# Sums of squares in column halves on GpSimd, the middle statistic one weight unit later, and the last out-projection tile earlier in VectorE's order

## The reference

```
y = xf * lax.rsqrt(jnp.mean(xf * xf, axis=-1, keepdims=True) + RMS_EPS)
x = x + 0.5 * (jax.nn.silu(h @ w_gate) * (h @ w_up)) @ w_down      # h = y * g
```

## Time and profile before

| what | value |
|---|---|
| runs of the kernel | 1577.7, 1579.8, 1580.04 us; median 1579.8 |
| the profiled execution's own time | 1578.12 us |
| its span in the profile | 1576.3 us |
| granted clock, mean | 0.976 of full speed |
| TensorE busy | 1486.0 us (94%), 7230 matmuls |
| VectorE, ScalarE, GpSimd busy | 569.3, 508.9, 765.7 us |

### The profile page before, as it was taken

One profiled execution on the slowest core, in us unless ns is written; L12 is line 12 of the kernel. 1 busy time (PEld: TensorE's weight loads), 2 busy tenths in 40 slices (PEclk: granted clock), 3 DMA queues, 4 the chain that ended last, 5 costly groups with the idle time before them and its releaser, 6 DMA issues.

```text
span 1576.3 us, 20170 instructions
## 1 busy us (share of the span) xinstructions
PE 1486.0 (94%) x7230; PEld 1229.4 (78%) x7230; DVE 569.3 (36%) x794; ACT 508.9 (32%) x706; POOL 765.7 (49%) x1013
## 2 busy tenths in 40 slices
PE   5796999999999999999999999689999999999997
PEld 5674888888888788888888687578867888888887
DVE  6796342222002832222000746934544322221003
ACT  4425333333123333222212674022233332232112
POOL 0373465555555655554555636260045654555553
PEclk9898999999999999999999999879999999999999
DMA  8871234322232222322322222000022322223221
GB/s 316 320 267 41 94 133 147 106 93 94 95 105 80 94 95 91 106 93 93 104 96 94 71 76 72 14 1 1 1 67 81 134 85 101 94 92 106 94 80 54
DMA packets 44545, 156.90 MB, mean 100 GB/s; under 512 B 4944, under 2 KB 7376, under 8 KB 44240
## 3 DMA queue, kind: packets, MB, share of 16 engines
q1 hardware_dynamic: 44496, 156.22, 28.6%
HBM read 154.11 MB, written 2.10 MB: 99 GB/s over the span
## 4 chain that ended last, share of the span: by engine, by line
PE 78%; issue 9%; DVE 7%; POOL 4%; ACT 1%; DVEq 0%; POOLq 0%; ACTq 0%
PE ps L1562 23%; PE ps L1564 23%; PE ps L1563 23%; POOL w_lo L458 4%; DVE act_lo L1031 1%; DVE tri_p L1028 1%; DVE tri_x L1028 1%; PE ps L1922 1%; DVE xT L1031 1%; PE ps L1978 1%; DVE mid_sq L1031 0%; PE ps L1929 0%; PE ps L1935 0%; PE ps L1876 0%; PE ps L1982 0%
## 5 line engine op out<-in xcount | busy, mean ns | idle before, releaser
L458 POOL TENSOR_TENSOR w_lo<-raw,w_hi 128x256 fp32r<-128x256 f32 x932 | 698.2, 783 | 723.5 <-ACT w_hi L623 653.8
L1562 PE MATMUL ps<-act_hi,w_hi 128*128 128x512 f32 x1328 | 526.4, 396 | 15.9 <-DVE act_lo L1028 11.4
L1563 PE MATMUL ps<-act_lo,w_hi 128*128 128x512 f32 x1328 | 518.6, 391 | 0.0
L1564 PE MATMUL ps<-act_hi,w_lo 128*128 128x512 f32 x1328 | 518.2, 390 | 0.0
L623 ACT ACTIVATE w_hi<-raw 128x1024 fp32r<-128x1024 f32 x233 | 245.0, 1054 | 447.3 <-PE ps L1564 420.7
L1562 PEld LDWEIGHTS ps<-act_hi,w_hi 128*128 128x128 f32 x1328 | 250.1, 188 | 80.2 <-issue 13.7
L1564 PEld LDWEIGHTS ps<-act_hi,w_lo 128*128 128x128 f32 x1328 | 250.3, 188 | 52.7
L1563 PEld LDWEIGHTS ps<-act_lo,w_hi 128*128 128x128 f32 x1328 | 250.3, 189 | 52.6 <-issue 2.4
L1562 PE MATMUL ps<-hid_hi,w_hi 128*128 (+3 forms) x584 | 220.4, 377 | 9.3 <-DVE hid_lo L1031 6.0
L1563 PE MATMUL ps<-hid_lo,w_hi 128*128 (+3 forms) x584 | 219.8, 376 | 0.0
L1564 PE MATMUL ps<-hid_hi,w_lo 128*128 (+3 forms) x584 | 219.7, 376 | 0.0
(11 more groups left out here) (264 smaller groups left out, 1155.8 us busy)
## 6 DMA issues: line engine op xcount, KB each, us to landing
raw<-weight_units SPq DMA_DIRECT2D x233, 512.0 KB, 3.2
wm_ring<-mod_units SPq DMA_DIRECT2D x16, 512.0 KB, 6.1
wm_mid<-mod_units SPq DMA_DIRECT2D x16, 512.0 KB, 6.4
wm_early<-mod_units SPq DMA_DIRECT2D x8, 512.0 KB, 9.3
wm_late<-mod_units SPq DMA_DIRECT2D x8, 512.0 KB, 4.7
x_tok<-tokens SPq DMA_DIRECT2D x4, 512.0 KB, 5.2
xT<-tokens_by_channel SPq DMA_DIRECT2D x1, 2048.0 KB, 15.1
result<-act_out SPq DMA_DIRECT2D x16, 128.0 KB, 1.8
```

Of the source, the lines that this page charges most:

```text
L458: ins = nc.gpsimd.tensor_tensor(w_lo[:, slot, c], raw[:, slot, c], w_hi[:, slot, c].bitcast(f32), SUB)
L1562: nc.tensor.matmul(o, wh, xh, start=start, stop=False, **check)
L1563: nc.tensor.matmul(o, wh, xl, start=False, stop=False, **check)
L1564: return nc.tensor.matmul(o, wl, xh, start=False, stop=stop, **check)
```

## The change

Three edits. GpSimd's additions of squares behind stages 0 and 1 are issued as two column halves of 128x256, the first counted on a semaphore of its own, `sum_part`. The function that `ffn` calls between the first up units becomes a table of functions by place: the own statistics stay behind the second up unit, the middle statistic moves behind the third. In the out-projection's boundary VectorE adds the last tile after five low parts instead of seven, and ScalarE's copy of the next unit's weights moves behind the first two high parts.

```
+LOW_FIRST = 5
...
-                    nc.gpsimd.tensor_tensor(sumsq[:, :], sq_buf[:, 0, :] if m == 1 else sumsq[:, :], sq_buf[:, m, :], ADD).then_inc(s["nx_sum"], 1)
+                    for h in range(2):
+                        x = slice(h * HALF, (h + 1) * HALF)
+                        ins = nc.gpsimd.tensor_tensor(sumsq[:, x], sq_buf[:, 0, x] if m == 1 else sumsq[:, x], sq_buf[:, m, x], ADD)
+                        ins.then_inc(s["nx_sum"] if h else sem("sum_part"), 1)
...
-            high_n(U_OUT + KT - 1 + AHEAD)
             for m in range(KT):
+                if m == 2:
+                    high_n(U_OUT + KT - 1 + AHEAD)
                 x2_high(m)
...
-            for m in range(KT - 1):
+            for m in range(KT):
                 x2_low(m)
-            x2_new(KT - 1)
-            x2_low(KT - 1)
+                if m == LOW_FIRST - 1:
+                    x2_new(KT - 1)
             x2_sum(KT - 1)
...
-                        if first and q == 0 and stage > 0:
-                            mid()
+                            if first and stage > 0 and (q, h) in mid:
+                                mid[(q, h)]()
...
-            def mid_stats():
+            def own_stat():
 
                 after(s0["x_new"], KT)
                 stat(s0["nx_sum"], KT - 1)
+
+            def mid_stat():
                 stat(sem("mid_sum"), KT - 1, 7, mid_sq[:, :])
 
-            ffn(1, U_UP1, U_DN1, s0["nx_lo"], mid_stats)
+            ffn(1, U_UP1, U_DN1, s0["nx_lo"], {(0, 1): own_stat, (1, 0): mid_stat})
...
-            ffn(2, U_UP2, U_DN2, sem("x2_lo"), lambda: stat(sem("x2_sum"), KT - 1))
+            ffn(2, U_UP2, U_DN2, sem("x2_lo"), {(0, 1): lambda: stat(sem("x2_sum"), KT - 1)})
```

More of the change, by code:

```diff
@@ L1656, in ffn @@
                         up_pair(i, False)
-                    mid()
+                    mid["end"]()
                 with pe.Fori(4 if stage == 0 else 1, FT // 2) as i:
@@ L1743, in y_spread @@
                 last.then_inc(sem("y_bc"), 1)
-            ffn(0, U_UP0, U_DN0, sem("a_lo"), lambda: mod_columns(GT2))
+            ffn(0, U_UP0, U_DN0, sem("a_lo"), {"end": lambda: mod_columns(GT2)})
             s0, s1, s2 = (ffn_sems(i) for i in range(3))
-            def mid_stats():
+            def own_stat():
                 after(s0["x_new"], KT)
                 stat(s0["nx_sum"], KT - 1)
+            def mid_stat():
                 stat(sem("mid_sum"), KT - 1, 7, mid_sq[:, :])
-            ffn(1, U_UP1, U_DN1, s0["nx_lo"], mid_stats)
+            ffn(1, U_UP1, U_DN1, s0["nx_lo"], {(0, 1): own_stat, (1, 0): mid_stat})
             def decay_product(p):
```

## The result

The changed kernel is slower: the ratio of its runs to those of the kernel before is 1.0040, 95% interval 1.0029 to 1.0052 (18 runs each). The medians are 1581.27 against 1576.14 us, which alone gives 1.0033; 1576.14 is lower than the 1579.8 of the first three runs. The changed kernel's runs lie in two groups, eleven from 1578.3 to 1582.3 and seven from 1585.3 to 1589.2; the profiled one (1580.59) is of the lower group, and no trace shows what parts them. The forecast was 1582.7 us and slower with a chance of 0.53. The profiled execution has a span of 1578.7 us against 1576.3. One run of the kernel before in a later series, at 2096.57 us and a granted clock of 0.68, is left out of the ratios.

The account below looks back on a forecast made before the run. TensorE was taken to bound the kernel, so only its waits at three boundaries counted. The terms +4.2 + 2.2 - 0.5 - 0.5 - 1.7 = +3.7 us gave 1582.7 us, range 1579.5 to 1586.0.

Parts of the forecast that it names:

- The chain behind the middle statistic: First boundary: fourth up unit waits on a 6.50 us chain through ScalarE's queue, no longer covered by the third unit; +4.2 us.
- The named releaser: First boundary: GpSimd's `w_lo` would end the 5 to 6 us of idle time before the fourth up unit.
- nothing else is late next: First boundary: VectorE's reciprocal and gate products, ScalarE's later copies and GpSimd's low parts shift equally, adding no further wait.
- The clock: Fourth up unit: after nearly 6 us idle, TensorE's first 3.0 to 5.7 us run at half rate; +2.2 us.
- The halves: First two boundaries: GpSimd's split sums hold VectorE's low parts for less time; -0.5 us at each.
- about 1.1 per low part, 1.89 per tile: VectorE at the first boundary: low parts wait only for the running half-sum, so a tile takes 1.89 us, not 1.96.
- The rival that GpSimd becomes the bound: Split sums give nothing and the third unit's low part is 0.6 us late; +5.5, 1584.5 us, chance 0.08.
- The last tile: Out-projection to third stage: adding the eighth tile after five low parts removes most of TensorE's wait; -1.7 us.
- The sum: Whole kernel: all predicted gains and losses together make it 3.7 us slower.
- The clock did not stay up: Rival for the fourth up unit: TensorE's clock does not fall after the idle stretch; +1.5, 1580.5 us, chance 0.13.
- The fast one: Rival at the first boundary: fourth unit's low part is ready, so the 1.68 us wait vanishes; -4.4, about 1574.6 us, chance 0.06.

Follow-up runs that it names:

- e2_mid: Kernel before with only the middle statistic moved behind the third up unit; ratio 1.0038 to the kernel before.
- e5_mid_filler: Kernel before with the middle statistic moved behind the third up unit, then 20 matmuls nobody reads in the idle stretch; ratio 1.0015 to the kernel before.
- e1_halves: Kernel before with only GpSimd's sums of squares split into column halves; ratio 1.0001 to the kernel before.
- e9_three_copies: Changed kernel with whole sums, fourth and fifth units' weight copies ahead of both roots, the sixth's between them; ratio 0.9976 to the kernel before.
- e7_tile_hoist: Kernel before with the earlier last out-projection tile and fourth and fifth units' weight copies ahead of the roots, middle statistic unmoved; ratio 0.9991.
- e3_last_tile: Kernel before with only the last out-projection tile added earlier and its weight copy moved; ratio 0.9985 to the kernel before.

## Why the prediction was right, and where it was not

- **The chain behind the middle statistic (+4.2 us).** Right. Measured +3.96 from own statistic to fourth unit (12.70 against 8.74), 4.0 with the filler. The named releaser and the queue are shown: with the copies moved, the fourth unit does not wait. That nothing else is late next was right for the change as it is. With the chain mended, the fifth unit was late next, by VectorE's gate product, and the sixth by ScalarE's copy in `up_pair`.
- **The clock (+2.2).** Right. Measured 2.1 between e2_mid and e5_mid_filler; the fourth unit itself is 1.9 us longer in the changed kernel and 2.1 in e2_mid.
- **The halves (-0.5 and -0.5).** Wrong in size. The step that failed is "about 1.1 per low part, 1.89 per tile", with the low part "started some 0.15 after the half". The half and the low part start 0.07 us apart (506.58 and 506.65), so the low part waits for nearly the whole half: 1.2 us, 2.03 per tile, against 2.00 before (the prediction's 1.89 and 1.96 each leave out one of the tile's two gaps of 0.04). From the first low part to the last new tile VectorE gained 0.4 us (505.03 to 513.98 against 504.07 to 513.42), not 0.8, and that all from the first low part. Then the last two low parts, which the prediction charged with 0.3, took 0.58 more (2.35 against 1.77). So the own statistic comes 0.16 us later behind the first unit (12.64 against 12.48), which a shorter wait for `mid_sq` gives back in e1_halves. At the second boundary GpSimd's last sum starts 0.27 us earlier behind the first unit instead of 0.7, and takes 0.14 more; the statistic comes 0.14 earlier. The rival that GpSimd becomes the bound is near the truth for this term, since GpSimd has hardly a pause left, but not in its price: the third unit's low part was not late.
- **The last tile (-1.7).** Right: -1.6 to -1.85 against the kernels without it, no wait in its place.
- **The sum (+3.7).** The measured ratio is +0.29 to +0.52%, 4.6 to 8.2 us. With the terms as measured the sum is +4.3: the halves, together 0.0 to -0.2 instead of -1.0, add about 0.9, the chain and its clock, 5.9 to 6.05 instead of 6.4, take 0.4 to 0.5 off, and the last tile adds 0.1. That the forecast's 1582.7 comes within 1.5 us of the median 1581.27 is partly luck: the forecast started from 1579.0, 2.9 us above the kernel before's 1576.14, and its step was too small, by 1.4 us by the medians (5.1) and by 2.6 by the ratio (6.3). The sign and the main term are no luck.
- **The rivals.** The clock did not stay up. The fast one, that the chain is hidden, needs the weight copies ahead of the roots (e9_three_copies), which the change does not do.

## What to carry to other kernels

Before a statistic is moved behind more work, follow what hangs on it through every in-order queue: here ScalarE's next instruction behind the root was a weight copy for a unit that TensorE would then need at once. The wait that went cost 1.7 us and was named by the profile; the cover that went with it was a 6.5 us chain that showed as no wait at all, because it had ended just in time. And where two engines hold each other up on SBUF, as GpSimd's sums and VectorE's low parts do here, cutting an instruction of one in two need not speed up the other: the second half now waited for the low part, the pauses of 0.88 and 0.52 us were used up, and a tile took 2.03 us instead of 2.00.

## What the runs showed of the hardware that was not expected

- In e7_tile_hoist the granted clock was down right behind a wait of 1.93 us (0.59 over the 4 us from 529), while it stayed at 1.00 behind waits of 0.96 to 1.22 us in the same place (before, e1_halves, e3_last_tile). This is one execution of each. The 0.7 us of longer wait came with 2.2 us of lost time.
- GpSimd's sums and VectorE's low parts take turns also within a pair of back-to-back GpSimd instructions: of two equal halves the first takes 0.74 us, and the second, which a low part holds up, 1.19. VectorE's addition of the down product, with one input in PSUM, is not held up (0.75).
- The recurrence between second and third boundary differs by up to 4.7 us from one profiled execution to the next in kernels that hardly differ there (316.9 to 321.6), with the mean granted clock at 0.95 in the shortest and 0.93 in the longest.
